# Loading and rounding x and the first two weight units of a float32 transformer kernel in smaller pieces from two queues, with a finer order of waits in the first products

## The reference, cut to what matters

```
h = x + 0.5 * (silu(n(x) @ w_gate) * (n(x) @ w_up)) @ w_down      # n(x) = x * rsqrt(mean(x*x) + eps) * gain
# x: 256 x 1024, w_gate and w_up: 1024 x 2816, w_down: 2816 x 1024
```

## Time and profile before

| | us |
|---|---|
| median of 3 runs | 1111.11 (1110.59 to 1111.15) |
| the profiled execution, its own time | 1111.75 |
| its span | 1110.0 |
| PE busy | 1104.7 |
| DVE busy | 789.0 |
| ACT busy | 620.8 |

### The profile page before, as it was taken

The page is one execution under the profiler, slowest core; times in us unless marked ns, Lnnn a source line. Parts: engine busy times, 40 slices in busy tenths (PEclk is TensorE's granted clock), DMA queues, the critical chain, the costliest instruction groups (busy, mean ns, idle before and its releaser), DMA issues.

```text
span 1110.0 us, 14873 instructions
## 1 busy us (share of the span) xinstructions
PE 1104.7 (100%) x5824; PEld 940.9 (85%) x5824; DVE 789.0 (71%) x1130; ACT 620.8 (56%) x823; POOL 65.0 (6%) x136
## 2 busy tenths in 40 slices
PE   9999999999999999999999999999999999999998
PEld 8888888888888888888888888888887788888887
DVE  6777754667987677775477787557999786777742
ACT  5656542677566456554356556337797854656530
POOL 2200000100000000000000000011342000000000
PEclk9999999999999999999999999999999999999999
DMA  9965555654454655555565555557643355555540
GB/s 312 309 195 190 190 190 190 211 168 136 167 194 160 201 190 190 190 190 190 191 208 190 190 190 190 190 151 252 234 151 124 145 184 165 191 189 194 190 178 38
DMA packets 142549, 207.97 MB, mean 187 GB/s; under 512 B 9280, under 2 KB 100568, under 8 KB 142480
## 3 DMA queue, kind: packets, MB, share of 16 engines
q1 hardware_dynamic: 139408, 198.07, 53.2%
q0 software_dynamic: 3056, 8.95, 2.4%
q10 hardware_dynamic: 16, 0.00, 0.0%
HBM read 205.93 MB, written 2.65 MB: 188 GB/s over the span
## 4 chain that ended last, share of the span: by engine, by line
PE 97%; DVE 1%; ACT 1%; DMA 0%; issue 0%; SPq 0%; ACTq 0%; DVEq 0%
PE banks L1815 28%; PE banks L1701 16%; PE banks L1703 16%; PE banks L1702 16%; PE banks L1812 14%; PE banks L1773 1%; PE banks L1723 1%; PE banks L2047 1%; PE banks L1984 1%; DMA raw<-in_ffn_w_gate 0%; DVE w_lo L1145 0%; PE banks L2077 0%; PE banks L2143 0%; PE banks L2074 0%; PE banks L2017 0%
## 5 line engine op out<-in xcount | busy, mean ns | idle before, releaser
L1145 DVE TENSOR_TENSOR w_lo<-raw,w_hi 128x2048 fp32r<-128x2048 f32 x186 | 423.5, 2280 | 167.0 <-ACT w_hi L756 166.7
L756 ACT ACTIVATE w_hi<-raw 128x2048 fp32r<-128x2048 f32 x186 | 352.2, 1897 | 110.9 <-PE banks L1703 107.6
L1815 PE MATMUL banks<-xT,w_hi 128*128 128x512 f32 x1344 | 314.4, 390 | 0.0
L1815 PEld LDWEIGHTS banks<-xT,w_hi 128*128 128x128 f32 x1344 | 249.1, 188 | 49.6
L1701 PE MATMUL banks<-w_hi,xT 128*128 128x512 f32 (+1 forms) x432 | 170.5, 395 | 0.0
L1812 PEld LDWEIGHTS banks<-xT,w_lo 128*128 128x128 f32 x1344 | 167.2, 192 | 3.3
L1812 PE MATMUL banks<-xT,w_lo 128*128 128x256 f32 x1344 | 169.5, 283 | 0.0
L1703 PE MATMUL banks<-w_hi,xT 128*128 128x512 f32 (+1 forms) x432 | 167.1, 387 | 0.0
L1702 PE MATMUL banks<-w_lo,xT 128*128 128x512 f32 (+1 forms) x432 | 166.8, 386 | 0.0
L834 ACT ACTIVATE gate<-gate 128x256 f32<-128x256 f32 x84 | 35.1, 418 | 182.9 <-DVE gate L1269 182.9
L1701 PE MATMUL banks<-w_hi,hT_hi 128*128 128x512 f32 x352 | 137.3, 390 | 0.0
(11 more groups left out here) (317 smaller groups left out, 901.1 us busy)
## 6 DMA issues: line engine op xcount, KB each, us to landing
raw<-in_ffn_w_gate SPq DMA_DIRECT2D x88, 512.0 KB, 3.7
raw<-in_ffn_w_up SPq DMA_DIRECT2D x88, 512.0 KB, 4.7
raw<-in_ffn_w_down SPq DMA_DIRECT2D x88, 512.0 KB, 4.1
raw<-in_w_in SPq DMA_DIRECT2D x76, 512.0 KB, 4.4
raw<-in_w_out SPq DMA_DIRECT2D x16, 512.0 KB, 3.9
raw<-in_w_branch_moba SPq DMA_DIRECT2D x4, 512.0 KB, 4.3
raw<-in_w_branch_sb SPq DMA_DIRECT2D x4, 512.0 KB, 4.9
raw<-in_w_branch_a SPq DMA_DIRECT2D x4, 512.0 KB, 3.7
```

The costliest lines, as they stand in the source:

```text
L756: act.activation(w_hi[u % SLOTS][:, 0:n], raw[u % RAWS][:, 0:n], ACT.Copy).then_inc(hi_done, 1)
L1145: dve.tensor_tensor(w_lo[r][:, 0:n], raw[r][:, 0:n], w_hi[u % SLOTS][:, 0:n], ALU.subtract).then_inc(lo_done, 1)
L1815: m = pe.matmul(bank[b + s], mh, xT[:, k].rearrange("p a s -> p (a s)"), start=first, stop=k == KC - 1, skip_group_check=c == 0)
```

## The change

x (1 MB) comes in four transfers instead of two, and each of the four halves of units 0 and 1 in two instead of one. The pieces of x, 256 columns each, are first on SyncE's queue; the identity, the gain row and the gate half of unit 0 (two pieces) are issued by ScalarE's queue; the up half of unit 0 and unit 1 stay on SyncE's queue in pieces. ScalarE and VectorE round them piece by piece, the second piece of turned x by VectorE. TensorE turns four pieces of x at a time instead of eight, and does the terms of `first_columns` in the order of `first_term` below. The second batch of zeros has two instead of three. GpSimd issues its loads of positions and biases behind `hi_done` 4. `pair_chunk` waits for `hi_done`, and for `lo_done` only ahead of its w_lo products.

The diff, cut to its core (`first_columns`, removed, was the loop described above):

```diff
+WARM = (5, 2, 1)
 
...
+        def load_first(eng, u, s, i, signal):
+
+            w = a[ffn_w[0][s]].rearrange("(k p) (c n) -> p k c n", p=P, n=CH)
+            k = 4 * u + 2 * i
+            eng.dma_start((gate_half, up_half)[s](raw[u])[:, 2 * i:2 * i + 2, :], w[:, k:k + 2, 0, :]).then_inc(signal, 16)
+
+        def first_bank(k):
+
+            return bank[3][:, 0:SEQ] if k == 1 else bank[4 + k // 2][:, k % 2 * SEQ:(k % 2 + 1) * SEQ]
+
         block = ctx.enter_context(nc.Block())
...
-            def load_x(n):
-
-                c = slice(n * NB, (n + 1) * NB)
-                sp.dma_start(x[:, :, c], a["x"][0].rearrange("(t p) d -> p t d", p=P)[:, :, c]).then_inc(x_in[n], 16)
+            def load_x(j):
+
+                c = slice(2 * j * P, 2 * (j + 1) * P)
+                sp.dma_start(x[:, :, c], a["x"][0].rearrange("(t p) d -> p t d", p=P)[:, :, c]).then_inc(x_in[j], 16)
...
-            sp.dma_start(ident, a["consts"][:, 0:P]).then_inc(ident_in, 16)
-            load_x(0)
+            for j in range(2):
+                load_x(j)
+            for i in range(2):
+                load_first(sp, 0, 1, i, up_in[i])
+            for j in range(2, 4):
+                load_x(j)
+            for i in range(2):
+                load_first(sp, 1, 0, i, gate_in[1][i])
+            for i in range(2):
+                load_first(sp, 1, 1, i, raw_in[1])
...
 
-            for n in range(2):
-                pool.wait_ge(x_in[n], 16)
+            for j in range(4):
+                pool.wait_ge(x_in[j], 16)
             pool.memset(freq[:, 0:1], INV_FREQ[0]).then_inc(gained, 4)
+            pool.wait_ge(hi_done, 4)
...
@@ -656,7 +674,6 @@
             m.then_inc(freq_set, 1)
             pool.dma_start(bias_cols, a["rel_bias_2"].rearrange("b h -> h b"), allow_slow_non_contiguous=True)\
                 .then_inc(table_in, 16)
-            pool.wait_ge(hi_done, 4)
             pool.dma_start(const[:, P:C_ONE], a["consts"][:, P:C_ONE]).then_inc(const_in, 16)
...
                 u0 = BASE[ph]
                 if ph == "F0":
                     act.wait_ge(gain_copied, 1)
-                    for u in range(2):
-                        if u == 0:
-                            first_x_hi(0)
-                            first_x_hi(1)
-                        else:
-                            act.wait_ge(first_half[1], 16)
-                            act.activation(gate_half(w_hi[1]), gate_half(raw[1]), ACT.Copy).then_inc(first_half_hi[1], 1)
-                            first_x_hi(2)
-                            first_x_hi(3)
-                        act.wait_ge(raw_in[u], landed(u))
-                        act.activation(up_half(w_hi[u]), up_half(raw[u]), ACT.Copy).then_inc(hi_done, 1)
+                    def gate_hi(u, i):
+                        k = slice(2 * i, 2 * i + 2)
+                        act.wait_ge(gate_in[u][i], 16)
+                        act.activation(gate_half(w_hi[u])[:, k, :], gate_half(raw[u])[:, k, :], ACT.Copy)\
+                            .then_inc(first_half_hi[u], 1)
+
+                    first_x_hi(0)
+                    act.wait_ge(first_half_hi[0], 1)
+                    gate_hi(0, 1)
+                    first_x_hi(1)
+                    for i in range(2):
+                        act.wait_ge(up_in[i], 16)
+                        act.activation(up_half(w_hi[0])[:, 2 * i:2 * i + 2, :], up_half(raw[0])[:, 2 * i:2 * i + 2, :],
+                                       ACT.Copy).then_inc(hi_done if i else up_hi, 1)
+                    for i in range(2):
+                        first_x_hi(2 + i)
+                        gate_hi(1, i)
+                    act.wait_ge(raw_in[1], landed(1))
+                    act.activation(up_half(w_hi[1]), up_half(raw[1]), ACT.Copy).then_inc(hi_done, 1)
                 else:
...
             act.preload_act_table_set("silu_and_others")
+            act.dma_start(ident, a["consts"][:, 0:P]).then_inc(ident_in, 16)
             act.dma_start(gain_rows, a[gains[0]].rearrange("(k p) -> k p", p=P)).then_inc(gain_row_in, 16)
+            for i in range(2):
+                load_first(act, 0, 0, i, gate_in[0][i])
             ffn("F0")
             mixer(0)
...
+                    def gate_lo(u, i):
+                        k = slice(2 * i, 2 * i + 2)
+                        dve.wait_ge(first_half_hi[u], i + 1)
+                        dve.tensor_tensor(gate_half(w_lo[u])[:, k, :], gate_half(raw[u])[:, k, :], gate_half(w_hi[u])[:, k, :],
+                                          ALU.subtract).then_inc(first_half_lo, 1)
+
+                    dve.wait_ge(gate_in[0][0], 16)
+                    dve.tensor_copy(gate_half(w_hi[0])[:, 0:2, :], gate_half(raw[0])[:, 0:2, :]).then_inc(first_half_hi[0], 1)
+                    dve.wait_ge(second_turned, 1)
+                    dve.tensor_scalar(xT_hi[:, 1, :], first_bank(1), gain_cols[:, 1:2], None, ALU.mult).then_inc(second_hi, 1)
+                    for i in range(2):
+                        gate_lo(0, i)
+                        if i == 0:
+                            dve.wait_ge(second_hi, 1)
+                        first_x_lo(i)
+                    for i in range(2):
+                        k = slice(2 * i, 2 * i + 2)
+                        dve.wait_ge(hi_done if i else up_hi, 1)
+                        ins = dve.tensor_tensor(up_half(w_lo[0])[:, k, :], up_half(raw[0])[:, k, :], up_half(w_hi[0])[:, k, :],
+                                                ALU.subtract)
+                        ins.then_inc(lo_done if i else up_lo, 1)
+                    first_x_lo(2)
+                    first_x_lo(3)
+                    for i in range(2):
+                        gate_lo(1, i)
+                    dve.wait_ge(hi_done, 2)
+                    dve.tensor_tensor(up_half(w_lo[1]), up_half(raw[1]), up_half(w_hi[1]), ALU.subtract).then_inc(lo_done, 1)
                     return
                 order = ("r0", "r1", "r2", "l0", "l1", "r3", "l2", "l3") if quarters(ph) == Q_MIX else \
...
+            def first_term(u, s, i, term):
+
+                j = 2 * u + i
+                if term == 0:
+                    pe.wait_ge(xT_hi_done, j + 1)
+                    if s == 0:
+                        pe.wait_ge(first_half_hi[u], i + 1)
+                    elif u == 0 and i == 0:
+                        pe.wait_ge(up_hi, 1)
+                    else:
+                        pe.wait_ge(hi_done, u + 1)
+                elif term == 1:
+                    if s == 0:
+                        pe.wait_ge(first_half_lo, j + 1)
+                    elif u == 0 and i == 0:
+                        pe.wait_ge(up_lo, 1)
+                    else:
+                        pe.wait_ge(lo_done, u + 1)
+                else:
+                    pe.wait_ge(xT_lo_done, j + 1)
...
-                    first_columns(1, 1)
+                    first_term(0, 0, 0, 1)
+                    first_term(0, 0, 0, 2)
+                    for term in range(3):
+                        first_term(0, 0, 1, term)
+                    first_turn(2)
+                    first_term(0, 1, 0, 0)
+                    first_term(0, 1, 1, 0)
+                    first_turn(3)
+                    first_term(0, 1, 0, 1)
+                    first_term(0, 1, 1, 1)
+                    first_term(0, 1, 0, 2)
+                    first_term(0, 1, 1, 2).then_inc(unit_used, 1)
+                    for s in range(2):
+                        for term in range(3):
+                            for i in range(2):
+                                m = first_term(1, s, i, term)
+                    m.then_inc(unit_used, 1)
                     return
                 turn_x(ph, 1)
                 batch(0, 0)
@@ -1830,12 +1892,13 @@
             def pair_chunk(ph, c):
 
                 u = BASE[ph] + 2 * c
-                pe.wait_ge(lo_done, u + 1)
+                pe.wait_ge(hi_done, u + 1)
                 for p in range(2):
                     pair_free(ph, c, p)
                     pair_products(ph, c, 0, p, False)
                 if c == 1 and ph not in FIRST_OF:
                     spread_rows(ph)
+                pe.wait_ge(lo_done, u + 1)
                 for p in range(2):
                     m = pair_products(ph, c, 0, p, True)
                 m.then_inc(unit_used, 1)
```

More of the change, by code:

```diff
@@ L95, in landed @@
     n = sum(DMAS + (v in (NARROW, NARROW + 1)) for v in range(u % RAWS, u + 1, RAWS))
[L96 removed]
+    return 16 * (n - (2 if u % RAWS == 0 else 0))
 Y_AT = [(37, 38, 40, 42), (37, 38, 40, 43)]
@@ L327, in build @@
         tile_done = sem("tile_done")
-        first_half = [sem("first_half0"), sem("first_half1")]
+        gate_in = [[sem(f"gate_in{u}{i}") for i in range(2)] for u in range(2)]
+        up_in = [sem("up_in0"), sem("up_in1")]
+        up_hi = sem("up_hi")
+        second_turned = sem("second_turned")
+        second_hi = sem("second_hi")
+        up_lo = sem("up_lo")
         gain_row_in = sem("gain_row_in")
@@ L334, in build @@
```

(69 more changed lines are left out.)

39 lines of the change are left out of this document (4 added, 35 removed).

## The result

The changed kernel takes 1112.83 us (median of 20 runs, 1111.51 to 1115.11), the kernel before 1110.88 (20 runs, 1110.59 to 1111.54): ratio 1.0017, 95% interval 1.0011 to 1.0024. It is 1.95 us slower, and its times spread over 3.6 us where those of before spread over 1. The forecast was 1110.4, and 1109.4 to 1111.4 for the range.

What follows compares the result with a forecast made beforehand. Bound: TensorE, busy 1104.7 of 1110.0 us; in the head, the chain from unit 2's landing to the hidden values, with 0.3 slack. Gain 0.46 + 0.2 = 0.66, so 1111.11 - 0.7 = 1110.4 us, range 1109.4 to 1111.4.

Steps and rivals of the forecast that it cites:

- First product: Start of TensorE's products in the head: claimed at 6.3 us, 1.7 earlier than 7.99.
- The floor of 6.0: Earliest first product by TensorE's own sequence: zeros to 3.55, gain row, two zeros, four turned pieces, one zero.
- the sign of being wrong: In the profile after, a first product past 7.2 us would show the forecast of 6.0 to 6.6 wrong.
- rival D: Thinner work ahead of the products keeps TensorE slow: chunk 1 at 22.55, time 1112.7 us; chance 0.10.
- Its sign: For rival D, in the profile after: loads of 0.2 us among products behind 7.5 us.
- TensorE's work behind it: From first product to chunk 1: 12.91 + 0.45 + 0.5 - 0.3 us, so chunk 1 at 19.85, 1.05 earlier.
- `pair_chunk`: At chunk 1, the old wait for unit 2's rests would keep 0.6 of the 1.05 us gain, the new none.
- Where the stall goes: TensorE reaches the hidden values at 25.3 us, before they are ready at 26.07 - d, and waits there.
- d: How much earlier unit 2 lands: 0.44 - 0.23 = 0.2 us, between -0.5 and 0.6.
- 0.46 + d: Gain past the hidden values: TensorE goes on at 26.55 - d against 27.01; with d 0.2, 0.66 us.
- The base of the forecast: Median of the kernel before, 1111.11 us, from which 0.7 was taken to get 1110.4.

Runs made afterwards that it cites:

- experiment 5: The changed kernel run again, nothing altered: 1113.07 us, ratio 1.0016.
- experiment 6: The changed kernel with unit 0's two gate pieces on SyncE's queue, each behind its piece of x: 1111.67 us, ratio 1.0007.
- experiment 9: The changed kernel with all loads on SyncE's queue, identity first, only the gain row on ScalarE's: 1110.72 us, ratio 0.9998.
- experiment 12: The changed kernel with the gate pieces on SyncE's queue and seven zeros instead of five ahead of the gain row: 1110.47 us, ratio 0.9996.
- experiment 11: The kernel before with the new wait of pair_chunk alone: 1110.96 us, ratio 1.0001.
- experiment 15: The changed kernel with all loads on SyncE's queue except the gain row, a second time (as experiment 9): 1110.63 us, ratio 0.9999.
- experiment 1: The changed kernel with seven zeros instead of five ahead of the gain row: 1111.59 us, ratio 1.0006.
- experiment 2: The kernel before with three zeros instead of five ahead of the gain row: 1111.66 us, ratio 1.0006.
- experiment 10: The kernel before with its identity moved to ScalarE's queue, ahead of the gain row: 1112.15 us, ratio 1.0012.
- experiment 13: The kernel before with its identity moved to ScalarE's queue, behind the gain row: 1113.20 us, ratio 1.0020.
- experiment 7: The kernel before with 20 zeros instead of five: 1113.21 us, ratio 1.0020.
- experiment 8: The changed kernel with 20 zeros instead of five: 1113.10 us, ratio 1.0020.
- experiment 14: The changed kernel with all loads on SyncE's queue except the gain row, and pair_chunk's old wait: 1111.27 us, ratio 1.0003.
- experiment 4: The changed kernel with pair_chunk's old wait, for the rests ahead of the products with rounded weights: 1111.93 us, ratio 1.0012.

## Why the prediction was wrong

**First product: this is the step that failed.** I had it at 6.3 (bounds 6.0 to 7.15) "since two queues run at once, about one more piece of SyncE's queue lands beside" what is needed. That takes the two queues for equals. The floor of 6.0 from TensorE's own order starts the gain row at 3.55, at the end of the zeros, though the change moves the identity, which it needs, to the second queue: its landing was put at no delay, without a reason. Measured: the gain row at 4.39 and the first product at 7.64 in the changed kernel (4.45 and 7.87 in its second profile), past the 7.2 that I had named as the sign of being wrong. The identity landed 3.1 us after issue instead of 1.9, and ScalarE's queue had 16.5% of the engines from 3 to 5 us. With all on one queue the same pieces give 5.64 and 5.78. Of the 2.14 us by which chunk 1 missed the forecast (21.99 against 19.85), 1.34 are the first product and 0.80 lie behind it.

The second queue, as the change uses it, costs 2.1 to 2.4 us of the median. In steps it is 1.4 for the gate pieces (experiments 5 to 6) and 0.95 for the identity (6 to 9), but the second step can also be had by two zeros (12), so it is a cost by way of the pause. No row of the kernel before shows SyncE's and ScalarE's queues busy at once, since ScalarE's held the gain row alone: I had nothing to size this term by, and gave it no rival. The only warning was that the stretch from 2 to 3 us, with the identity and the start of x, moved no more than 131 GB/s.

**TensorE's pace.** I gave rival D 0.10 and priced it at 1112.7; it is nearly what happened, by another way in: not by thinner work ahead of the first product as such, but by two pauses that the late landings make (0.83 us at 3.6 and 0.57 before the first product). Its sign, loads of 0.2 us among products behind 7.5, is there. The loads take their shorter time from about 7.6 us on in the kernel before (6.0 in experiment 11), from 10.9 and 12.9 in the changed one, and from 4.5 and 4.8 with the same thin work on one queue (experiments 9 and 15). Filling the first pause with zeros is worth 1.2 us in both heads with a second queue (experiments 1 and 12), and making one in the kernel before costs 0.75 (experiment 2). The two causes aren't separate sums: part of what the queue costs is paid by way of the pace. How much of it, these runs leave open; experiments 10 and 13 show losses of 1.27 and 2.3, in which the first products are at full pace and chunk 1 is late by 0.65 and 1.7.

**TensorE's work behind it.** I had 19.85 for chunk 1 with the first product at 6.3. On one queue it was 5.64 and 19.82, and 5.78 and 19.26: right in size. From the first product to chunk 1 that is 14.18 and 13.48 us, where I had 13.55. That the order and the pieces cost nothing that can be measured is shown by experiments 7 and 8, and by 9 and 15.

**`pair_chunk`.** The 0.6 us of the earlier trace rows is what experiment 14 shows at chunk 1 (a wait of 0.61), and nothing in the kernel before (experiment 11) or the changed one (4). That the hidden values would swallow nearly all of it was wrong: by the medians 0.64 reached the end, by the profiles about 0.3.

**Where the stall goes, and d.** The changed kernel never reached it: its chunk 1 was too late, though unit 2 landed about 0.1 us earlier than before (issued at 7.55, 8.6 us to landing). On one queue TensorE stood for the hidden values as forecast (0.83 us), went on with unit 3's rests at 26.4 and 26.56 (forecast 26.35), and unit 2's rounding began at 16.18 and 16.33, so d was 0.07 and -0.08, not 0.2. The forecast of 0.46 + d for that version comes to 0.4 to 0.5; the medians are 0.16 and 0.26 below the kernel before, with intervals of the ratio that hold 1. So this version is level with the kernel before or 0.2 us faster, which these runs can't tell apart; experiment 12, with its median 0.4 below, is no clearer. The 0.2 for d was meant for two queues, and there d was larger where x and the gate pieces shared SyncE's queue: 0.5 in experiment 6 (unit 2 at 15.72 instead of 16.25) and 0.8 in experiment 10 (15.45), the last above my bound of 0.6. The base of the forecast was off as well: it was a median of three runs, 1111.11, where 20 runs have 1110.88.

## What to carry to other kernels

Before a transfer is moved to a second queue, ask what it is needed for and what runs beside it: a small transfer that stands first on the only queue lands in its own time, and beside a large one on another queue it can take twice as long (3.1 to 4.6 us instead of 1.9), here with everything waiting for it. What stands behind it on that queue comes later still, be it 4 KB. When TensorE's start is moved, look at the pauses ahead of it, since a pause of under 1 us can cost as much again in pace; such a loss can show as a spread of the times. And price an early start by the chain that hangs on landings, not by TensorE's own.

## What was not expected of the hardware

The identity, 64 KB in rows of 512 bytes, took 1.8 to 2.0 us to land when it stood first on SyncE's queue with x behind it, and 3.0 to 4.6 us on ScalarE's queue beside x on SyncE's: 3.0 to 3.6 beside pieces of x with 1 KB rows, 3.6 and 4.6 beside 2 KB rows. The same second queue had half of the engines from 5 to 7 us. Why it got 16.5% from 3 to 5 stays open. In one execution the granted clock went back to 0.50 for 3.3 us in the middle of the products, after TensorE had stood for some 1.7 us [experiment 1].
